# Hybrid mLSTM / attention / mixture-of-experts block: expert units of 32 places in four column groups, and a rebuilt router

## The reference

```python
probs = softmax(xt @ w_router); sel = probs + router_bias
group_score = max(sel.reshape(-1, 4, 4), -1); top_group = argmax(group_score)
_, idx = top_k(where(in_group, sel, NEG), 2)
w = probs[idx] / sum(probs[idx])
for e in range(16):
    h = silu(xt @ w_gate[e]) * (xt @ w_up[e])
    y = y + combine[:, e:e + 1] * (h @ w_down[e])
h = layer_norm(ALPHA * h + y, ln2_g, ln2_b)
```

## Time and profile before

| | |
|---|---|
| median of 3 runs | 842.73 us (841.73 to 843.7) |
| the profiled execution's own time | 843.29 us |
| its span, first to last instruction | 841.0 us |
| TensorE matmul busy | 785.0 us, 93% |
| VectorE / ScalarE busy | 344.8 us, 41% / 242.5 us, 29% |
| bytes moved | 251.28 MB, mean 299 GB/s |
| granted TensorE clock, mean | 0.990 |

### The profile page before, as it was taken

One profiled execution on the slowest core, in us unless ns is written; L12 is line 12 of the kernel. 1 busy time (PEld: TensorE's weight loads), 2 busy tenths in 40 slices (PEclk: granted clock), 3 DMA queues, 4 the chain that ended last, 5 costly groups with the idle time before them and its releaser, 6 DMA issues.

```text
span 841.0 us, 12805 instructions
## 1 busy us (share of the span) xinstructions
PE 785.0 (93%) x4566; PEld 472.4 (56%) x4567; DVE 344.8 (41%) x765; ACT 242.5 (29%) x527; POOL 23.6 (3%) x49
## 2 busy tenths in 40 slices
PE   4999999999999999998999999998999989989983
PEld 3998679998889999873333332332333323323331
DVE  6676446554666778463222211220222202202225
ACT  2454423445666655231111011101110111011100
POOL 2002000000001000000000000000000000000000
PEclk9999999999999999999999999999999999999997
DMA  8965040555013544955999999999999999999991
GB/s 249 386 231 200 4 197 1 199 199 200 2 43 159 200 180 149 394 227 212 372 429 427 429 428 428 429 428 427 429 426 427 430 425 429 428 427 429 425 396 50
DMA packets 36219, 251.28 MB, mean 299 GB/s; under 512 B 5377, under 2 KB 12626, under 8 KB 22882
## 3 DMA queue, kind: packets, MB, share of 16 engines
q1 hardware_dynamic: 34128, 249.71, 72.5%
q10 hardware_dynamic: 2066, 1.25, 0.5%
HBM read 249.91 MB, written 1.05 MB: 298 GB/s over the span
## 4 chain that ended last, share of the span: by engine, by line
PE 67%; DMA 24%; DVE 4%; ACT 2%; issue 2%; POOL 1%; DVEq 0%; POOLq 0%; SPq 0%; ACTq 0%
DMA raw<-in_w_up_e_dram 24%; PE ps L1895 24%; PE ps L1562 8%; PE ps L1563 7%; PE ps L1564 7%; PE ps L1847 2%; PE ps L1855 2%; PE ps L1537 1%; PE ps L1618 1%; PE ps L1614 1%; PE ps L1674 1%; PE ps L1862 1%; PE ps L1791 1%; PE ps L1793 1%; PE ps L1792 1%
## 5 line engine op out<-in xcount | busy, mean ns | idle before, releaser
L1895 PE MATMUL ps<-raw,xg 128*64 128x512 f32 x640 | 146.2, 605 | 17.9 <-DMA raw<-in_w_up_e_dram 12.5
L1562 PE MATMUL ps<-hi_h,whi 128*128 128x256 f32 (+1 forms) x448 | 129.6, 289 | 2.6 <-DVE wlo L968 2.5
L1564 PE MATMUL ps<-hi_h,wlo 128*128 128x256 f32 (+1 forms) x448 | 127.4, 284 | 0.0
L1563 PE MATMUL ps<-lo_h,whi 128*128 128x256 f32 (+1 forms) x448 | 127.2, 284 | 0.0
L1895 PE MATMUL ps<-raw,hid 128*64 128x512 f32 x512 | 113.4, 595 | 0.0
L968 DVE TENSOR_TENSOR wlo<-raw,whi 128x512 fp32r<-128x512 f32 x144 | 93.5, 691 | 47.1 <-ACT whi L667 44.4
L1895 PEld LDWEIGHTS ps<-raw,xg 128*64 128x64 f32 x640 | 45.6, 139 | 115.2 <-issue 85.7
L1562 PEld LDWEIGHTS ps<-hi_h,whi 128*128 128x128 f32 x448 | 84.4, 188 | 7.2 <-DVE wlo L968 3.7
L667 ACT CAST whi<-raw 128x512 fp32r<-128x512 f32 (+1 forms) x144 | 83.3, 619 | 13.6 <-PE ps L1564 11.9
L1489 DVE TENSOR_TENSOR gs<-ps,gsig 128x512 f32<-128x512 f32 x16 | 11.1, 692 | 183.8 <-ACT gsig L915 183.8
L1564 PEld LDWEIGHTS ps<-hi_h,wlo 128*128 128x128 f32 x448 | 84.5, 189 | 0.0
(11 more groups left out here) (311 smaller groups left out, 975.0 us busy)
## 6 DMA issues: line engine op xcount, KB each, us to landing
raw<-in_w_down_e_dram SPq DMA_DIRECT2D x32, 2048.0 KB, 21.7
raw<-in_w_up_e_dram SPq DMA_DIRECT2D x24, 2048.0 KB, 24.7
raw<-in_w_gate_e_dram SPq DMA_DIRECT2D x16, 2048.0 KB, 23.4
gate_x<-in_w_gate_e_dram SPq DMA_DIRECT2D x16, 2048.0 KB, 23.2
raw<-in_w_in_dram SPq DMA_DIRECT2D x28, 1024.0 KB, 9.2
up_x<-in_w_up_e_dram SPq DMA_DIRECT2D x16, 1024.0 KB, 27.5
raw<-in_w_branch_m_dram SPq DMA_DIRECT2D x4, 1024.0 KB, 8.1
raw<-in_w_branch_a_dram SPq DMA_DIRECT2D x4, 1024.0 KB, 8.0
```

The lines of the kernel that those rows point to most:

```text
L1562: mm(o, w1, hi[:, k, c0:c0 + n], start=(k == 0), stop=False)
L1563: mm(o, w1, lo[:, k, c0:c0 + n], start=False, stop=False)
L1564: last = mm(o, w2, hi[:, k, c0:c0 + n], start=False, stop=(k == KB - 1))
L1895: last = mm(ps[r0:r0 + SLOTS, bank_no, :], lhs[:, k % 4, k // 4, :], w[:, k % 2, 512 * c:512 * c + 512], start=(k == 0), stop=(k == KB - 1))
```

## The change

- `SLOTS` becomes 32. The 32 places are the stationary operand in one of four column groups of the array (`CG` = 4), and each group has 256 output columns (`CW`). A row block of a product is 4 matmuls of 256 columns where it was 2 of 512. For gate, up and gather the columns of a group are pairs of neighbours, one pair out of every four columns of a half (`group_columns`). Two transposes, where there were four, turn the rows. Scatter is 8 matmuls of 32 rows and 256 columns where it was 4 of 64 rows and 512.
- The up matrix has two whole places: `up_x_left`, `up_x_right0`, `up_x_right1`. All of up 1 is issued before the router is done. The order of transfers is written anew.
- The normalisation and the layer norm's gain are folded into the router: gain into `wr`, mean and bias as corrections by column sums. The "out" section runs by column half; the first half's residual, transposes and logits come before the last piece. Gain and bias are put on the gathered rows (`take_gathered`, two operations).
- The selection compares pairs; rank counting is in bf16. `acc` is started by VectorE in 8 operations instead of by ScalarE in 2. The gain and bias rows for it are broadcast by TensorE, and the last layer norm's rows are loaded at the end by SyncE.

```diff
-SLOTS = 64
+SLOTS = 32
+CG = P // SLOTS
+CW = D // CG
...
+    def group_columns(rows, c):
+        return rows.rearrange("p (h i q a) -> p h q i a", h=2, q=2, a=2)[:, c // 2, c % 2]
...
-        for q, (read, n) in enumerate(((s.pieces_used, OUT_BASE + PIECES + NBUF), (s.h1_back, 2 * TT))):
-            sp.wait_ge(read, n)
-            sp.dma_start(flat(up_x[q][:]), flat(four_rows(w_up[0, 1], 0)[:, 2 * q:2 * q + 2, :])).then_inc(up_x_in[q], 16)
+        sp.dma_start(flat(up_x_right[1][:]), flat(four_rows(w_up[0, 1], 1)[:, 2:4, :])).then_inc(up_x_in[2], 16)
+        sp.wait_ge(s.pieces_used, OUT_BASE + PIECES + NBUF)
+        sp.dma_start(flat(up_x_left[:]), flat(four_rows(w_up[0, 1], 0))).then_inc(up_x_in[0], 16)
+        sp.dma_start(flat(up_x_right[0][:]), flat(four_rows(w_up[0, 1], 1)[:, 0:2, :])).then_inc(up_x_in[1], 16)
...
+        def fetch_up(e, odd):
+            last = last_block(e - 2)
+            sp.wait_ge(s.up_used, last * 4 + 2)
+            if odd:
+                sp.dma_start(flat(up_x_left[:]), flat(expert_rows(w_up, e, 0))).then_inc(up_x_in[0], 16)
+                for j in range(2):
+                    sp.wait_ge(s.up_used, last * 4 + (j + 3))
+                    sp.dma_start(flat(up_x_right[j][:]), flat(expert_rows(w_up, e, 1)[:, 2 * j:2 * j + 2, :])
+                                 ).then_inc(up_x_in[1 + j], 16)
...
+        with sp.Fori(0, NE // 4 - 1) as i:
+            for odd in range(2):
+                fetch_gate(i * 2 + (2 + odd), odd)
+                fetch_up(i * 2 + (2 + odd), odd)
+                fetch_down(i * 2 + (1 + odd))
+        fetch_gate(NE // 2, False)
+        with sp.Fori(NE // 4 - 1, NE // 2 - 2) as i:
+            for odd in range(2):
+                fetch_down(i * 2 + (1 + odd))
+                fetch_up(i * 2 + (2 + odd), odd)
+                fetch_gate(i * 2 + (3 + odd), not odd)
+        fetch_down(NE - 3)
+        fetch_up(NE - 2, False)
         fetch_gate(NE - 1, True)
-        fetch_rest(NE - 1, True)
+        fetch_down(NE - 2)
+        fetch_up(NE - 1, True)
+        fetch_down(NE - 1)
...
+        l1g = chan[:, C_L1G:C_L1G + KB].unsqueeze(2).to_broadcast([P, KB, NE])
+        own(dve.tensor_tensor(wr_b[:], wr[:], l1b, ALU.mult))
+        own(dve.tensor_tensor(wr[:], wr[:], l1g, ALU.mult))
...
+        def take_gathered(n):
+            dve.tensor_tensor(xg[:], ps[:, B_XT, 0:CW].rearrange("p (a c s) -> p a c s", c=CG, s=SLOTS), by_slot(gain4),
+                              ALU.mult).then_inc(s.xg_scaled, 1)
+            dve.wait_ge(s.xg_scaled, n)
+            dve.tensor_tensor(xg[:], xg[:], by_slot(bias4), ALU.add).then_inc(s.xg_ready, 1)
...
+        for t in range(TT):
+            for c in range(2):
+                cols = slice(512 * c, 512 * c + 512)
+                own(dve.scalar_tensor_tensor(out=acc[:, t, cols], in0=ps[:, 6 + c, :], scalar=ALPHA,
+                                             in1=h1[:, t, cols], op0=ALU.mult, op1=ALU.mult))
...
+            if n == PIECES - 2:
+                pe.wait_ge(evac[WM], KB + 2)
+                pe.wait_ge(evac[WA], KB + 2)
+                turn_half(0)
+        logits(0)
+        turn_half(1)
+        logits(1).then_inc(s.logit_done, 1)
...
-                        for c in range(2):
+                        for c in range(CG):
                             r0 = SLOTS * c
-                            last = mm(ps[r0:r0 + SLOTS, bank_no, :], lhs[:, k % 4, k // 4, :],
-                                      w[:, k % 2, 512 * c:512 * c + 512], start=(k == 0), stop=(k == KB - 1))
+                            o, cols = ps[r0:r0 + SLOTS, bank_no, 0:CW], w[:, k % 2, CW * c:CW * c + CW]
+                            if j < 2:
+                                o, cols = pairs_of(o), group_columns(w[:, k % 2, :], c)
+                            last = mm(o, lhs[:, k % 2, k // 2, :], cols, start=(k == 0), stop=(k == KB - 1),
+                                      tile_position=(0, r0))
```

More of the change, by code:

```diff
@@ L126, in build @@
     ahead_b = perm("ahead_b", [P, P], BF16)
-    before = perm("before", [P, P])
-    ones = perm("ones", [P, P])
-    slotno = perm("slotno", [P, 2, SLOTS])
+    before_b = perm("before_b", [P, P], BF16)
+    one = perm("one", [P, 1])
+    one_b = perm("one_b", [P, 1], BF16)
+    first = perm("first", [P, EPG, EPG])
+    crow = perm("crow", [81, P])
+    gain4 = perm("gain4", [P, 2, 4])
+    bias4 = perm("bias4", [P, 2, 4])
+    rout_b = perm("rout_b", [P, NE])
+    nmr = perm("nmr", [P, TT])
+    slotno = perm("slotno", [P, CG, SLOTS])
     sel_at = top[0]
@@ L191, in build @@
     ahead = at("ahead", [P, P], F + 38560)
+    before = at("before", [P, P], F + 39072)
     SCAN = 2 * P
@@ L238, in build @@
     unit_of = at("unit_of", [1, 2, UNITS], F + 20544, I32)
[L239 to L242, removed]
-    gate_x = at("gate_x", [P, KB, D], F + 31264)
[L244 to L251, removed]
+    total = at("total", [1, 1], F + 20864, I32)
+    table_load = at("table_load", [1, 1], F + 20896)
+    unit_f = at("unit_f", [1, 2, UNITS], F + 20928)
+    passed = at("passed", [1, UNITS, NE], F + 16896)
+    over = at("over", [1, NE, MAXBLK], F + 21248)
+    gate_x = at("gate_x", [P, KB, D], F + 31264)
+    up_x_left = at("up_x_left", [P, 4, D], 0)
+    up_x_right = (at("up_x_right0", [P, 2, D], split_area + 8192 - work),
+                  at("up_x_right1", [P, 2, D], F + 23072))
+    zsb = at("zsb", [P, CW], 17408)
+    xg = at("xg", [P, 2, CG, SLOTS], 17408 + 4096)
+    pick = at("pick", [P, TT, P], 17408 + 6144)
+    wpick = at("wpick", [P, TT, P], 17408 + 7168)
+    wpt = at("wpt", [P, TT, P], 16384)
+    rows1 = at("rows1", [P, 2, D], F + 31264)
     ps = nc.alloc_psum_tensor("ps", [P, 8, 512], F32)
@@ L561, in _ @@
         own = Steps(pool, s.pool)
-        for t, v in ((ident, 0.0), (late, 0.0), (ahead, 0.0), (before, 1.0), (sel, 0.0), (ones, 1.0),
+        for t, v in ((ident, 0.0), (late, 0.0), (ahead, 0.0), (before, 1.0), (sel, 0.0), (one, 1.0), (one_b, 1.0), (first, 0.0),
                      (minus_half, -0.5)):
@@ L741, in _ @@
         act.wait_ge(s.consts, 1)
-        for narrow, wide in ((ident_b, ident), (late_b, late), (ahead_b, ahead)):
+        for narrow, wide in ((ident_b, ident), (late_b, late), (ahead_b, ahead),
+                             (before_b, before)):
             act.copy(narrow[:], wide[:]).then_inc(s.masks_ready, 1)
@@ L883, in _ @@
             split_out(n)
[L885 to L892, removed]
+        for b in range(4):
+            if b == 2:
+                act.activation(table_load[:], neglam[0:1, :], ACT.Exp)
+            act.wait_ge(s.ht_t1, b + 1)
+            act.copy(ht[:, 2 * b:2 * b + 2, :], turned1[:, 2 * b:2 * b + 2, :]).then_inc(s.ht_ready, 1)
         act.wait_ge(s.router_exp, 1)
@@ L896, in _ @@
                            bias=rt[:, 15, t:t + 1], accum_out=rt[:, 15, 4 + t:5 + t]).then_inc(s.exp_r, 1)
+        act.wait_ge(s.nmr_ready, 1)
         for t in range(TT):
[L899 to L907, removed]
+            act.activation(h1[:, t, :], h1[:, t, :], ACT.Identity, bias=nmr[:, t:t + 1],
+                           scale=rstd[:, t:t + 1]).then_inc(s.h1_ready, 1)
         act.wait_ge(s.gath_done, 1)
-        act.copy(xsb[:], ps[:, B_GATH, :]).then_inc(s.xsb_ready, 1)
+        act.copy(xsb[:], ps[:, B_GATH, 0:CW]).then_inc(s.xsb_ready, 1)
         act.wait_ge(s.units_ready, 1)
@@ L1510, in _ @@
             pick_tokens(e2, b2)
+        for c in range(CG):
+            dve.wait_ge(s.scat_done, count * 4 + (c + 1))
+            add_group(c)
         for t in range(TT):
[L1512 to L1517 removed]
+            variance(t, acc, lambda half: (s.acc_added, count * 4 + (2 * half + 6)), s.fin_var)
         dve.wait_ge(s.rows2_in, 32)
@@ L1686, in _ @@
         stream(QA, hi_h, lo_h, META, None)
+        pe.wait_ge(s.rout_in, 1)
+        mm(ps[:, 7, 0:2 * NE], one[:].to_broadcast([P, P]), rout_sum[:].rearrange("p a e -> p (a e)"), start=True,
+           stop=True).then_inc(s.rout_done, 1)
         stream(VA, hi_h, lo_h, 0, (evac[KA], KB + 2), KB - 2)
@@ L1783, in _, with turn_half, logits @@
         stream(WA, ya_hi, ya_lo, 0, (evac[GB], KB + 2))
+        def turn_half(half):
+            for t in range(TT):
+                pe.wait_ge(s.resid_done, TT * half + t + 1)
+                for k in range(4 * half, 4 * half + 4):
+                    last = pe.transpose(turned1[:, k, P * t:P * t + P], h1[:, t, P * k:P * k + P], ident[:])
+                    if t == TT - 1 and k % 2:
+                        last.then_inc(s.ht_t1, 1)
+        def logits(half):
+            for k in range(4 * half, 4 * half + 4):
+                pe.wait_ge(s.ht_ready, max(k // 2 + 1, 2))
+                for t in range(TT):
+                    last = mm(ps[:, t, 0:NE], ht[:, k, P * t:P * t + P], wr[:, k, :], start=(k == 0), stop=(k == KB - 1))
+            return last
         for n in range(PIECES):
-            k, half = divmod(n, 2)
-            pe.wait_ge(s.mg_lo_s, k + 1)
```

(27 more changed lines are left out.)

359 lines of the change are left out of this document (180 added, 179 removed).

## The result

The changed kernel takes 881.3 us (median of 4 runs, 878.44 to 883.63) against 842.65: 1.0455 times the time before, 95% interval 1.0421 to 1.0488. The profiled execution took 879.49 us, its span is 877.7 us, and the mean granted clock 0.926 where it was 0.990.

What follows compares the result with a forecast made beforehand. Weight transfers at 428 GB/s were taken to bound the kernel: restart 391.3 + bytes 421.4 + ramp 4.7 + three stalls of 7.3 + 1.7 = last landing 844.4, + 32.7 = 877 span, 879 us; 8 in 10: 858 to 908.

Steps and rivals of the forecast that it cites:

- Restart: Time when weight transfers resume after the router, waiting for expert 0's second unit: 391.3 us, 5.4 later than before.
- Unit 0: First unit of expert 0: 13.5 us plus 3.3 for the scatter waiting on VectorE's pick and acc start.
- Cost of a unit: TensorE time per 32-place unit: 13.5 us against 25.9, if four column groups run as two do, product 3.43.
- The first rival: Four column groups don't run side by side at full rate: 991 us at no gain, 892 in milder form; chance 0.17.
- Gaps: Empty transfer queue at experts 1, 3 and 6, gate waiting behind down: 7.3 us each plus 1.7 clock; 4.7 at restart.
- the ramp: Slow start of transfers at the restart, a lone transfer being slower than a full queue: 4 to 5 us, 4.7 summed.
- The clock's 1.7 in each: Lower granted clock doubling a half product where TensorE is waited for: 1.7 us in each of three transfer stalls.
- After the last landing: Half of down 15 1.7, clock 1.7, expert 15's second unit 13.5, tail 15.8: 32.7 us, where it was 20.6.
- All second units together: Cost of experts needing two units: 57 us, with expert 0 16.8, experts 1, 3, 6 9 each, expert 15 13.5.
- That the stalls don't appear: Rival: queued transfers cover the stalls at experts 1, 3 and 6, but units 0 and 15 cost as said; 852, chance 0.08.
- that the rest cancels: Rival: the transfers bound both ends and everything else cancels; 840 to 845 us, chance 0.03.
- The one on the other side: Rival: routing on the chip lets experts fit one unit each, restart at 374.5; 822 us, 2.5% faster; chance 0.04.

Runs made afterwards that it cites:

- the order's run: Changed kernel with only the transfer order altered: down of e, up of e+1, gate of e+2 from the first expert on; 857.67 us, ratio 1.0195.

## Why the prediction was right

The time, 879 us forecast and 881.3 measured, and the sign were right, and the mechanism was: second units hold up the restart, the queue and the end. But part of the closeness is luck, errors that cancel. The last landing was forecast at 844.4 and measured at 844.40, from a restart 4.6 too early and gaps 4.6 too long.

- **Restart: 391.3 forecast, 395.93 measured**, 4.6 too early. The step that failed is the router's: I let the ranks follow the mask and gave the broadcasts of gain and bias and the fillers no time, nor this stage a low clock. The ranks came 5 us after the mask (370.4 against 365.4). At the full clock broadcasts and fillers would have ended at some 367.3, an estimate from 3.74 us for the broadcasts where they ran at the full clock and 5.97 us for 52 filler records before; so some 3 of the 5 us are the clock's. All ten traces of the changed kernel and its variants have the clock at 0.50 to 0.62 from 362 to 366 us, though TensorE was busy for 3.5 of the 4 us from 358 to 362; the kernel before has 1.00. Why it falls there, no run settles. Moving the broadcasts gave 3.5 us at the restart.
- **Unit 0: 16.8 forecast, 17.0 measured** (376.7 to 393.7), and this too is luck. I gave VectorE's `pick` and start of `acc` 3.3 us; TensorE waited for VectorE 1.5. Another 1.45 is the gate product, 5.15 us at a granted clock of 0.68 where it takes 3.70 at the full one. In the run with the broadcasts moved, at the full clock, the wait is 1.95 and the unit takes 16.1.
- **Cost of a unit: 13.5 forecast, 14.1 measured.** Four groups run side by side. A product is 3.70 us at full clock for 64 records, 57.8 ns each, where 3.43 was forecast; 1.86 times as fast as with two groups, out of 2. The Trainium skill gives 2.38 times for three groups (TensorE: Matmul & The Clock Gate, Part 3), which as an estimate would make 4.3 here; the measurement is nearer to the full gain, and it decides. The first rival fell.
- **Gaps: 27 for the three breaks and 4.7 for the ramp forecast, 27.1 for both measured** (448.5 from the first issue to the last landing, less 421.4). The breaks lie where they were said to lie, at experts 1, 3 and 6, and none later. Their empty times are 5.5, 7.6 and 5.3 us; the undoing of the order gave 20.8 between restart and last landing, 6.9 for each where 9.0 was forecast, and leaves 6.3 for the ramp and the rest. The clock's 1.7 in each was too much: it was low in one of three, 0.67, and 1.00 in the others. That is some 3 of the 4.6 us which cancelled the restart's.
- **After the last landing: 32.7 forecast, 33.3 measured**, the last unit among it; taking it away gave 12.8. All second units together were forecast at 57 and measured at 52.5.
- **The rivals.** That the stalls don't appear is refuted by the trace and by the order's run, and that the rest cancels (840 to 845) by the time. The one on the other side, one unit for every expert, was made true by hand: 828.76 us where it gave 822, and on the faster side as it said; the restart came at 382.5, 8 us later than I had it there.

Why TensorE's gain was not seen is thus shown: 24 units at 14.1 are 338 us and 16 at 25.9 are 414, both under 470 us of transfers, and a second unit holds three things: the place of a matrix that the queue wants next, the first restart, and the end. The same 24 units with another order, other experts first and last and the broadcasts moved took 836.23 us.

## What to carry to other kernels

Where weights stream for the whole stage, a cheaper unit is worth nothing by itself: ask how long each one keeps its place in the buffers, and what stands behind the last landing. Halving the block makes a second pass over the same matrices, and the order of one queue must be right for one pass and for two; the order that takes 24 us off the one costs the other 9. When work on TensorE is added to a stage that VectorE's small steps set, look whether it stands ahead of a product that they wait for, and at which clock it runs there.

## What was not expected of the hardware

Four column groups of 32 with 256 float32 columns start every 57.8 ns (231 ns for four, where two groups of 512 columns take 0.43 us), some 8% over half. A transfer of 2048 KB issued into the empty queue (433.54) landed after 7.5 us here, the next beside it after 10.6. The clock fell in the router stage in every trace of the changed kernel, though TensorE was busy before it: 16 broadcast products took 5.73 to 7.17 us there and 3.74 at the full clock. Without fillers the gather and the turns behind the rank count ran at the lower level too (3.68 and 1.13 us for 1.94 and 0.75), so that 6.6 us of earlier ranks became 4 at the restart.
